# The experts' down bias in spare rows of the bias table, and 256 KB more of the first pair's weights beside the ring

## The reference, cut to what matters

```python
logits = (h @ w_router + b_router).astype(jnp.float32)
top_val, top_idx = lax.top_k(logits, TOP_K)
gates = jax.nn.softmax(top_val, axis=-1).astype(h.dtype)
...
def expert_block(args):
    xb, e = args
    g = xb @ w_gate[e] + b_gate[e]
    u = xb @ w_up[e] + b_up[e]
    g = jnp.minimum(g, SWIGLU_LIMIT)
    u = jnp.clip(u, -SWIGLU_LIMIT, SWIGLU_LIMIT)
    glu = g * jax.nn.sigmoid(SWIGLU_ALPHA * g)
    return ((u + 1.0) * glu) @ w_down[e] + b_down[e]
...
return jnp.zeros_like(h).at[row_tok].add(out * row_gate[:, None])
```

## Time and profile before

| what | us |
|---|---|
| median of 3 runs | 1100.98 (1100.59 to 1101.01) |
| the profiled execution, its own time | 1101.59 |
| its span, first to last instruction | 1099.8 |
| PE busy | 1045.9 |
| transfers | 438.24 MB, mean 398 GB/s over the span |

### The profile page before, as it was taken

How to read it: one execution, slowest core, us unless ns; L and a number is a source line. 1 busy time by engine, 2 the same in 40 slices (tenths; PEclk the granted TensorE clock), 3 DMA queues, 4 the chain that set the end, 5 groups by cost and what they waited for, 6 DMA issues and landing times.

```text
span 1099.8 us, 12728 instructions
## 1 busy us (share of the span) xinstructions
PE 1045.9 (95%) x5458; PEld 503.6 (46%) x5458; DVE 302.7 (28%) x622; ACT 130.9 (12%) x243; POOL 13.1 (1%) x18
## 2 busy tenths in 40 slices
PE   9999999999999999999899989999799989999896
PEld 8999996534433443344234423433243324343332
DVE  5977888420302121121112111030202011212022
ACT  2212250310000001001000010000000100000012
POOL 1200000000000000000000000000000000000000
PEclk9999999999999999999899999999899989999999
DMA  9974377999999999999999999999999999999996
GB/s 337 427 295 154 138 296 295 352 428 428 434 430 440 431 436 431 434 436 434 427 441 431 434 434 431 436 431 431 436 434 427 443 429 421 434 429 430 425 428 250
DMA packets 22771, 438.24 MB, mean 398 GB/s; under 512 B 4560, under 2 KB 5968, under 8 KB 9424
## 3 DMA queue, kind: packets, MB, share of 16 engines
q1 hardware_dynamic: 22160, 435.05, 93.2%
q10 hardware_dynamic: 576, 2.69, 0.6%
HBM read 436.28 MB, written 1.05 MB: 398 GB/s over the span
## 4 chain that ended last, share of the span: by engine, by line
PE 62%; DMA 35%; DVE 1%; issue 1%; ACT 1%; DVEq 0%; SPq 0%; POOL 0%; POOLq 0%
DMA ring<-in_experts 35%; PE ps L2133 26%; PE ps L2182 11%; PE ps L1688 8%; PE ps L2039 3%; PE ps L2191 2%; PE ps L1867 2%; PE ps L1683 2%; PE ps L1932 2%; PE ps L1737 1%; PE ps L2171 1%; PE ps L2048 1%; PE ps L2149 0%; ACT region_va L911 0%; PE ps L1809 0%
## 5 line engine op out<-in xcount | busy, mean ns | idle before, releaser
L2133 PE MATMUL ps<-ring,xT 128*64 128x512 f32 x2044 | 461.2, 607 | 26.1 <-DMA ring<-in_experts 26.1
L2133 PEld LDWEIGHTS ps<-ring,xT 128*64 128x64 f32 x2044 | 145.3, 139 | 314.2 <-issue 285.3
L2182 PE MATMUL ps<-ring,region_va 128*64 128x512 f32 x1024 | 227.2, 595 | 18.8 <-DMA ring<-in_experts 11.1
L2182 PEld LDWEIGHTS ps<-ring,region_va 128*64 128x64 f32 x1024 | 73.5, 137 | 150.9 <-issue 138.0
L1583 DVE TENSOR_SCALAR g<-ps 128x1024 f32<-128x1024 f32 x16 | 19.6, 1225 | 349.1 <-PE ps L2133 343.2
L1688 PE MATMUL ps<-ring 128*128 128x128 f32 x784 | 89.7, 276 | 0.1
L1688 PEld LDWEIGHTS ps<-ring 128*128 128x128 f32 x784 | 88.5, 192 | 0.9 <-DVE ring L997 0.3
L1605 DVE TENSOR_SCALAR region_va<-ps 128x512 f32<-128x512 f32 x32 | 22.1, 692 | 183.0 <-PE ps L2133 183.0
L1529 DVE TENSOR_TENSOR xT<-ps,g_ffn 128x512 f32<-128x512 f32 x30 | 20.7, 692 | 187.0 <-PE ps L2039 187.0
L2039 PEld LDWEIGHTS ps<-sel,x 128*128 128x128 f32 x480 | 55.4, 192 | 9.5 <-issue 9.5
L2191 PE MATMUL ps<-g,g_T 128*128 128x512 f32 x128 | 59.2, 605 | 0.0
(11 more groups left out here) (271 smaller groups left out, 548.3 us busy)
## 6 DMA issues: line engine op xcount, KB each, us to landing
ring<-in_experts SPq DMA_DIRECT2D x19, 4096.0 KB, 40.6
ring<-in_experts SPq DMA_DIRECT2D x28, 2048.0 KB, 12.4
ring<-in_head SPq DMA_DIRECT2D x13, 2048.0 KB, 15.8
ring<-in_experts SPq DMA_DIRECT2D x12, 1024.0 KB, 8.5
ring<-in_experts SPq DMA_DIRECT2D x7, 512.0 KB, 8.1
ring<-in_first SPq DMA_DIRECT2D x7, 384.0 KB, 6.9
ring<-in_experts ACTq DMA_DIRECT2D x2, 1024.0 KB, 9.1
ring<-in_experts SPq DMA_DIRECT2D x1, 1536.0 KB, 6.5
```

What stands on the lines that cost most here:

```text
L2133: last = mm(bank(banks + half)[rows, :], xT[:, 2 * m + c, rows], weights[:, k], start=False, stop=m == 3 and c == 1, skip_group_check=True)
L2182: last = mm(bank(first + half)[rows, :], hTm[:, 2 * m + c, rows], w[:, c, half, k], start=m == 0 and c == 0, stop=m == 3 and c == 1, skip_ ...
```

## The change

The down bias now comes as it is, 32 rows x 1024 floats (128 KB), into the 32 spare rows of `bias3` (`bd`), issued behind the last load of the head. The gates are written three times instead of four, two transposes put one half of the tokens each into rows 96 to 127, and all four products of `start_y` work on these rows. `start_y` moves behind the first load of the up matrix (load 4). The place in `r_va` takes 512 more columns of pair 0's load 3 (`aside_k`, 256 KB), so `ASIDE_FROM` falls from 3072 to 2560 columns, and 256 KB more of pair 1 are loaded during the head.

```diff
-ASIDE_LOAD, ASIDE_FROM = 3, 3 * D
+ASIDE_LOAD, ASIDE_FROM = 3, 3 * D - W512
...
+        BD = slice(3 * E, 4 * E)
+        bd = bias_r[BD, :].bitcast(F32)
...
-        g4 = gs_r[:, 0:P].rearrange("p (r e) -> p r e", e=E)
-        gates_T = gs_r[:, P:2 * P]
-        bd4 = r_va[:, 0:W512]
+        gates3 = gs_r[:, 0:3 * NT * E].rearrange("p (r n) -> p r n", r=3)
+        gates_T = gs_r[BD, :]
...
+        aside_k = r_va[:, 0:W512]
...
+            sp_.dma_start(bd, b_down).then_inc(ld_bd, 16)
             lower, upper = SLOT_OF.index(HEAD_SLOT[12]), SLOT_OF.index(HEAD_SLOT[13])
...
-            sp_.dma_start(aside, experts_v[0][:, ASIDE_LOAD * SLOT_COLS + ASIDE_FROM:(ASIDE_LOAD + 1) * SLOT_COLS]
-                          ).then_inc(aside_loaded, 16)
+            at = ASIDE_LOAD * SLOT_COLS
+            sp_.dma_start(aside, experts_v[0][:, at + 3 * D:at + SLOT_COLS]).then_inc(aside_loaded, 16)
             sp_.wait_ge(ssq2_ready, 4)
-            sp_.dma_start(bd4, b_down4).then_inc(ld_bd4, 16)
+            sp_.dma_start(aside_k, experts_v[0][:, at + ASIDE_FROM:at + 3 * D]).then_inc(aside_loaded, 16)
...
-            nc.scalar.copy(gates_T, bank(5)[:, 0:P]).then_inc(gates_T_ready, 1)
+            nc.scalar.copy(gates_T, bank(5)[BD, 0:NT * P]).then_inc(gates_T_ready, 1)
...
-                nc.tensor.transpose(bank(5)[:, 0:P], gs_r[:, 0:P], ident).then_inc(g4_done, 1)
+                for a in range(NT):
+                    lo = (1 - a) * E
+                    last = nc.tensor.transpose(bank(5)[:, a * P:(a + 1) * P], gs_r[:, lo:lo + P], ident)
+                last.then_inc(g4_done, 1)
...
-                pe.wait_ge(ld_bd4, 16)
-                for r in range(4):
-                    rows = slice(r * E, (r + 1) * E)
-                    last = mm(bank(Y_B + r), gates_T[rows, :], bd4[rows, :], start=True, stop=True)
+                pe.wait_ge(ld_bd, 16)
+                for a in range(NT):
+                    for half in range(2):
+                        last = mm(bank(Y_B + 2 * a + half), gates_T[:, a * P:(a + 1) * P],
+                                  bd[:, half * W512:(half + 1) * W512], start=True, stop=True)
...
-                        pe.wait_ge(aside_loaded, 16)
+                        pe.wait_ge(aside_loaded, 16 * 2)
...
+                        if first_pair and which == 1 and m == 0:
+                            start_y()
...
-                if first_pair:
-                    start_y()
                 gate_or_up(1, second)
```

More of the change, by code:

```diff
@@ L168, in build @@
 def build(nc, x_d, first_d, lam_q1, lam_k1, lam_q2, lam_k2, subln_g, norm_ffn_g, w_router, b_router, b_gate, b_up,
-          b_down4, norm_final_g, head_d, experts_d, const_d, out_d):
+          b_down, norm_final_g, head_d, experts_d, const_d, out_d):
     ctx = ExitStack()
@@ L224, in build @@
         logit_parts = sb("logit_parts", P)[:, :]
-        bias3 = sb("bias3", 2 * D, BF16)[:, :].rearrange("p (w n) -> p w n", w=2)
+        bias_r = sb("bias3", 2 * D, BF16)[:, :]
+        bias3 = bias_r.rearrange("p (w n) -> p w n", w=2)
+        BD = slice(3 * E, 4 * E)
+        bd = bias_r[BD, :].bitcast(F32)
         small = sb("small", 112)
@@ L399, in build @@
         ld_vectors, ld_router = sem("ld_vectors"), sem("ld_router")
-        ld_bd4, ld_gfin, ld_bias, ld_bias3 = sem("ld_bd4"), sem("ld_gfin"), sem("ld_bias"), sem("ld_bias3")
+        ld_bd, ld_gfin, ld_bias, ld_bias3 = sem("ld_bd"), sem("ld_gfin"), sem("ld_bias"), sem("ld_bias3")
         stored = sem("stored")
@@ L1557, in _ @@
             own.settle()
-            nc.vector.tensor_copy(g4.rearrange("p (a w) e -> p a w e", a=NT),
-                                  gx.unsqueeze(2).to_broadcast([P, NT, 2, E])).then_inc(g4_ready, 1)
+            nc.vector.tensor_copy(gates3, gx.rearrange("p a e -> p (a e)").unsqueeze(1).to_broadcast([P, 3, NT * E])
+                                  ).then_inc(g4_ready, 1)
             gathered_part((gat_done, 1), 2, xT_ready)
@@ L2131, in gate_or_up @@
                                 rows = slice(k * SLOTS, (k + 1) * SLOTS)
-                                weights = aside_w if first_pair and 4 * which + m == ASIDE_LOAD and c == half == 1 else w[:, c, half]
+                                weights = w[:, c, half, k]
+                                if first_pair and 4 * which + m == ASIDE_LOAD and c == 1:
+                                    weights = aside_w[:, k] if half else aside_k if k else weights
                                 last = mm(bank(banks + half)[rows, :], xT[:, 2 * m + c, rows],
-                                          weights[:, k], start=False,
+                                          weights, start=False,
                                           stop=m == 3 and c == 1, skip_group_check=True)
@@ L2319 @@
     give("b_up", a["b_up"])
-    b_down = a["b_down"]
-    give("b_down4", np.concatenate([b_down[:, 0:W512], b_down[:, W512:D]] * NT))
+    give("b_down", a["b_down"])
     give("norm_final_g", a["norm_final_g"])
```

## The result

The changed kernel takes 1106.1 us, the median of 5 runs (1104.15 to 1107.75), against 1100.59 us (1100.55 to 1101.01) for the kernel before on the same chip. The ratio is 1.0042, with a 95% interval of 1.0032 to 1.0053: it is slower by more than 0.2%, where 1101.1 us and a range of 1099.8 to 1102.7 were predicted. The profiled execution takes 1104.15 us, its span is 1102.4 us: 2.6 us more than the span before.

The account below looks back on a forecast made before the run. The prediction took the transfer stream, bytes over rate, as the bound while the queue never runs dry. Bytes -0.61 us and a late load 5 refill +0.75 us summed to +0.15 us, giving 1101.1 us, range 1099.8 to 1102.7.

Parts of the forecast that it names:

- the wait for load 3: PE at load 3, now in two pieces: the second lands about 9 us before PE comes, cost 0.
- the second transpose: PE, transposing the gates: one more 128 x 128 transpose adds 0.11 to 0.26 us, taken as 0.15.
- DVE's cover: DVE, first pair: its result, delayed by `start_y`, is ready at 233.5 us, 1.1 us before PE transposes it.
- The bias' own transfer: Behind the head's last load: 128 KB, 0.3 us at the stream's rate, hidden by an idle link, cost 0.
- The bytes: Load 3's refill is 256 KB shorter, taking 0.61 us off the full stream.
- So the late issue costs **+0.75 us: Load 5's refill, issued 2.7 us later, 1.5 us ahead of the previous landing, lands at 241.8 us; bounds 0 to +1.7.
- the queue grows from there: From load 6, issued 3.2 us ahead of load 5's landing: PE frees 2 MB per 3.5 us, the link needs 4.85.
- So it runs dry once at most: First refills: the queue empties at most once, at load 5's refill, with no further loss behind it.
- PE is the bound: Rival: PE's 2.7 us slip reaches the end, 1103.7 us; chance 0.05.
- The stream's rate changes: Rival: other transfer lengths and memory places shift the stream's rate by half a percent, 1097 or 1105 us; chance 0.07.
- The stream stays full: Rival: 1.5 us ahead is enough at load 5, only bytes count, 1100.4 us; chance 0.33, with or without overlap.
- the products still overlap: Rival: `start_y`'s four products overlap, slip 0.15 us, queue stays full, 1100.4 us; within the full stream's 0.33.

Follow-up runs that it names:

- e12: Kernel before, with only load 5's refill held on SP until load 6 is used as well: 1103.33 us, 1.002 against the kernel before.
- e1: Changed kernel run again, unaltered: 1104.65 us, 1.0035 against the kernel before.
- e8: e6 without the 256 KB piece, load 3 cut at 3072 columns as before: 1104.58 us, 1.0031 against the kernel before.
- e14: Changed kernel, unaltered, one more profiled execution: 1106.13 us.
- e16: Changed kernel, unaltered, one more profiled execution: 1104.13 us.
- e6: Changed kernel with `start_y` moved just ahead of the first `scatter`, gates' transposes in other spare rows: 1104.07 us, 1.0024 against the kernel before.
- e13: Changed kernel, unaltered, one more profiled execution: 1105.61 us.
- e15: Changed kernel, unaltered, one more profiled execution: 1104.28 us.
- e2: Kernel before with only `start_y`'s four products put in one row group and moved behind load 4, transfers unchanged: 1105.7 us, 1.0037 against the kernel before.
- e9: e6 with the bias products taken out of the first pair and added ahead of the 14th pair's scatter: 1100.94 us, 1.0002 against the kernel before.
- e3: Changed kernel with `start_y`'s products cut to 128 of their 512 columns: 1102.32 us, 1.001 against the kernel before.
- e4: Changed kernel with load 5's refill in two halves, the first issued when half the load is used: 1106.16 us, 1.0037 against the kernel before.
- e7: e6 with load 5's refill held on SP until load 6 is used: 1103.97 us, 1.0028 against the kernel before.
- e10: e9 without the 256 KB piece, load 3 cut at 3072 columns as before: 1102.48 us, 1.0009 against the kernel before.
- e11: e9 with load 5's refill in two halves: 1101.81 us, 1.0006 against the kernel before.
- e5: Changed kernel with `start_y`'s four products over all 128 rows of another buffer, same length: 1104.72 us, 1.0028 against the kernel before.

## Why the prediction was wrong

**What held.** The mechanism and its first place: the end is set by the stream, and the change touches it at load 5's refill. Step by step: the wait for load 3 is 0 (its second piece lands at 203.91 + 6.9 = 210.8 us, PE comes at 219.78); the second transpose costs 0.11 us, at the low end of 0.11 to 0.26; `start_y` takes 3.63 us; it ends at 231.12 us (231.2 predicted); DVE's cover holds with 1.2 us to spare (1.1 predicted); load 5's refill is issued at 234.74 us (234.66) and lands at 241.94 (241.8). The bias' own transfer lands 7.9 us after its issue at 101.10 us and nobody waits for it. The bytes left the stream: load 4 lands 1.09 us earlier, more than their 0.61; its own refill is issued 0.99 us earlier as well.

**The step that failed** is the term "So the late issue costs **+0.75 us**", bounds 0 to 1.7, with what it leans on: "the queue grows from there" and "So it runs dry once at most". The landing of load 5 itself was forecast within 0.15 us. What was wrong is to read the price of the dry spell from that landing, against the landing that a full stream would have given: behind a restart the 16 parts land within 0.6 us, in a full stream within 1.9, and that hides 1.3 us of idle link. Wrong as well was that the queue runs dry once at most. The runs show in its place: 2.2 us of stream lost ahead of load 5, where the sum had 0.75, then 0.7 us at load 6 and 1.3 us at the third pair's first refills, where the sum had nothing. e12 isolates the first without any change to PE: 2.6 us of stream, 2.1 us in the time.

**It could be read from the trace of before.** I took the first load into an idle link, at 132.16 and 160.45 us, and asked only when it lands. At both places a second load follows, issued at 136.02 and 162.24 us, 3.3 and 5.3 us ahead of the first one's landing. Stretches of before:

```profile
138.00:142.00 4.00, 4.00 (x39) 4.00 (x37) 3.67 (x11) 4.00 (x18) 0.00 (x0) 1.00 0.94 344
...
163.00:171.00 8.00, 8.00 (x74) 8.00 (x74) 7.90 (x11) 1.17 (x2) 0.00 (x0) 1.00 1.00 426
...
172.00:174.00 2.00, 2.00 (x21) 2.00 (x20) 1.93 (x4) 0.00 (x0) 0.00 (x0) 1.00 0.03 12
```

The last line shows that the link goes quiet well ahead of a landing: it moves 12 GB/s from 172 us on, and the load lands at 173.6. The first shows that 3.3 us ahead is not enough behind a restart (344 GB/s), the second that 5.3 us is (426 GB/s). Load 6 was forecast 3.2 us ahead.

**Why a landing can come late with the link full.** In the rows of after the second loads land 7.5 us (136.00 + 10.7 = 146.70, behind 132.13 + 7.1 = 139.23) and 6.0 us (162.21 + 11.4 = 173.61, behind 160.43 + 7.2 = 167.63) behind the first. Fifteen of their 16 parts are through by 145.2 and 172.5 us, and one comes 1.5 and 1.1 us later. The Trainium skill, "DMA: Bandwidth & Descriptors", section on why a DMA increments its semaphore by 16, says that a transfer runs on up to 16 engines that finish independently, and is complete only with the last of them. The trace agrees. Into each of these two loads falls one packet of 16 KB of the kind `instruction`, which takes 0.9 to 1.0 us on one of the 16; into load 6 of e12 fall two, and two of its parts land 1.5 and 1.9 us behind the first. That such a packet holds a part back fits these places, but in four other traces (e1, e8, e14, e16) one near the end of the same load, at 171.2 to 171.6 us, holds nothing back, and no run tests it.

**A step that was missing.** The prediction followed the slip to load 5 and stopped. The queue is shallow at more places: the kernel before issues load 6 5.75 us ahead of load 5's landing and the third pair's first refill 4.5 us ahead. A slip of 2.7 us goes into each of them until the stream falls behind PE; e6 shows that moving it by 23 us only chooses another one.

**The clock.** The prediction has no term for it. In e13 and e14 PE's granted clock falls behind `start_y`, load 5 takes 1.7 us longer, and the time is 1105.6 to 1106.1 us against 1104.1 to 1104.65 us in the four profiled executions of this kernel without it (after, e1, e15, e16). The mean granted clock of every run is on record and goes the same way: of the 14 executions of the changed kernel the six with 0.986 or more took 1104.0 to 1104.65 us, the eight with 0.985 or less 1105.6 to 1107.75 us. Four of the five runs behind the median of 1106.1 us are of the second kind. So the medians stand 5.5 us apart, while the executions of the first kind lie 2.5 to 3.6 us above the kernel before on the same chip, and the lost stream less the bytes came to 3.7. In e2, with the same slip, one run at 0.987 took 1105.82 us and breaks the order, so the clock is not all of the spread. It is not the loss itself either, which both kinds show.

**The rivals.** "PE is the bound" gave 1103.7 us, nearer than the forecast, by a mechanism that e9 and e12 rule out. "The stream's rate changes" gave 1105 us on its slow side, the nearest number; it falls with e2, and the stretches from 300 us on run within 2% of those of before. "The stream stays full" and "the products still overlap" are ruled out by the rows above.

## What to carry to other kernels

In a kernel bound by its stream, work added to the engine that releases buffers costs nothing where the queue is deep and several times the idle moment where it is shallow: find for every refill, not only the first, how long before the landing ahead of it it is issued. Here refills issued 0.7 to 1.2 us ahead cost 2 us of stream and more, those 3.2 to 4.0 us ahead in the changed kernel about 0.7 us each, and those of the kernel before, 4.4 us ahead and more, nothing. It is no sharp limit: in e3 a refill 3.8 us ahead kept the stream full, and one 4.7 us ahead did not. The price of a dry spell is read from the bytes moved over a stretch that holds it, not from the landing of the load that is late: that landing is the last of 16 parts, and behind a restart these lie closer together than in a full stream.

## What the hardware showed that was not expected

**A lower clock behind products over few rows.** When the four products over 32 rows run one behind another (3.63 us), the granted clock behind them falls to 0.50, the 1.2 GHz level, in some executions: near 230 us in four of eight profiles (e2, e4, e13, e14; not in after, e1, e15, e16), behind the same products near 258 us in all three (e6, e7, e8: `scatter` takes 5.33 us instead of 3.63), and near 985 us in all three (e9, e10, e11), where the same scatter takes 5.0 to 5.3 us and costs nothing. PE had no gap just ahead of any of these. It is not seen with the four products side by side in four row groups (before, 1.07 us), nor in e3 (1.08 us), nor in the one profile of e5 with all 128 rows. The same level stands in every trace at other places too. In that of before the clock falls near 542 us, where PE has waited 3.21 us for a load (the figure in brackets at the end of the line):

```profile
543.35 9.11 PE L2133 MATMUL ps<-ring,xT 128*64 128x512 f32 x28 [3.21 <-DMA ring<-in_experts]
```

The Trainium skill, "TensorE: Matmul & The Clock Gate", Part 1, says that the low level is the default and that activity releases it; the levels agree. Whether the few rows are the cause no run here settles, since e5's timed runs spread as widely.

**The landings of a stream** are told by the slowest of 16 parts, as told above: with the link full they keep 4.83 to 4.95 us apart, whatever lies between the first part and the last, and behind a restart they do not.
